# Mixture-of-experts start-up: the first unit's tokens by products with slot marks inside the router

## The reference

```python
def hierarchical_moe(h, w_rg, b_rg, w_re, b_re, w_e_gate, w_e_up, w_e_down):
    """h (T,D) -> (T,D). Top-1 group, then top-2 experts inside the chosen group."""
    p_grp = softmax(h @ w_rg + b_rg); g_sel = argmax(p_grp)
    le = (h @ w_re + b_re).reshape(T, N_GROUPS, E_PER_GROUP)   # 4 groups of 8
    top_p, top_e = top_k(softmax(le[g_sel]), 2)
    w_tok = p_g * top_p / sum(top_p)
    # every expert's tokens are packed into blocks of 128 rows, each block with one expert
    ys = (silu(xb @ w_e_gate[e]) * (xb @ w_e_up[e])) @ w_e_down[e]   # per block
    # out = sum over a token's two picks of weight * ys[row of the pick]
```

## Time and profile before

| what | value |
|---|---|
| three runs | 2894.31, 2905.34, 2900.13 us, median 2900.13 |
| the profiled execution | 2899.79 us, its span 2896.8 us |
| granted TensorE clock over the span | 0.943 |
| TensorE busy | 2591.6 us (89%) |
| VectorE busy | 2064.4 us (71%) |
| ScalarE busy | 926.9 us (32%) |
| GpSimd busy | 406.4 us (14%) |

### The profile page before, as it was taken

The page is one execution under the profiler, slowest core; times in us unless marked ns, Lnnn a source line. Parts: engine busy times, 40 slices in busy tenths (PEclk is TensorE's granted clock), DMA queues, the critical chain, the costliest instruction groups (busy, mean ns, idle before and its releaser), DMA issues. The chain is left out here.

```text
span 2896.8 us, 41643 instructions
## 1 busy us (share of the span) xinstructions
PE 2591.6 (89%) x16631; PEld 1948.6 (67%) x16631; DVE 2064.4 (71%) x2805; ACT 926.9 (32%) x981; POOL 406.4 (14%) x214
## 2 busy tenths in 40 slices
PE   5999888888999989998999997998884999999991
PEld 3444888547888754564788875886573788888870
DVE  6581576688777638536877666985755899999983
ACT  2201111122221013432222103333212777777761
POOL 1000000100000010000000000000001366666642
PEclk8999899899999999999999998999995999999995
DMA  5210222316664271201666323321305899999962
GB/s 190 87 59 18 80 91 76 133 52 189 181 195 132 87 237 65 73 30 58 201 184 183 129 87 108 88 87 44 145 14 221 309 364 367 365 362 356 357 238 104
DMA packets 241821, 459.57 MB, mean 159 GB/s; under 512 B 31398, under 2 KB 193726, under 8 KB 226329
## 3 DMA queue, kind: packets, MB, share of 16 engines
q1 hardware_dynamic: 220344, 432.09, 42.8%
q0 software_dynamic: 14368, 23.79, 2.4%
q10 hardware_dynamic: 6978, 1.80, 0.3%
HBM read 457.50 MB, written 30.56 MB: 168 GB/s over the span
## 5 line engine op out<-in xcount | busy, mean ns | idle before, releaser
L49 PE MATMUL ffn_bank<-ffn_xT_high,ffn_wi_high 128*128 128x512 f32 x704 | 278.4, 395 | 8.9 <-DVE ffn_wi_low L43 5.3
L50 PE MATMUL ffn_bank<-ffn_xT_low,ffn_wi_high 128*128 128x512 f32 x704 | 277.7, 394 | 0.0
L398 DVE SCALAR_TENSOR_TENSOR ffn_nsum<-ffn_nw,ffn_cond,ffn_nsum 128x256 f32<-128x256 f32 x336 | 162.9, 485 | 12.0
L2953 POOL DMA_INDIRECT expert_rows<-exp_ys,exp_to_row x32 | 155.7, 4867 | 45.1 <-issue 44.3
L49 PEld LDWEIGHTS ffn_bank<-ffn_xT_high,ffn_wi_high 128*128 128x128 f32 x704 | 134.0, 190 | 39.2 <-DVE ffn_wi_low L43 6.0
L43 DVE TENSOR_TENSOR moe_g_low<-moe_g,exp_g_high 128x4096 fp32r<-128x4096 f32 x32 | 141.6, 4426 | 25.7 <-ACT exp_g_high L3027 25.7
L50 PEld LDWEIGHTS ffn_bank<-ffn_xT_low,ffn_wi_high 128*128 128x128 f32 x704 | 133.6, 190 | 28.1
L43 DVE TENSOR_TENSOR moe_u_low<-moe_u,exp_u_high 128x4096 fp32r<-128x4096 f32 x32 | 141.6, 4425 | 13.5 <-ACT exp_u_high L3027 13.5
L3027 ACT CAST exp_g_high<-moe_g 128x4096 fp32r<-128x4096 f32 x32 | 116.4, 3636 | 105.1 <-PE exp_p_g L51 79.5
L49 PE MATMUL ffn_bank<-ffn_wo_high,ffn_act_high 128*128 128x512 f32 x352 | 137.8, 392 | 4.8 <-DVE ffn_wo_low L43 4.8
L43 DVE TENSOR_TENSOR moe_d_low<-moe_d,exp_d_high 128x4096 fp32r<-128x4096 f32 x32 | 141.4, 4419 | 0.0
(11 more groups left out here) (646 smaller groups left out, 6217.9 us busy)
## 6 DMA issues: line engine op xcount, KB each, us to landing
moe_g<-in_w_e_gate SPq DMA_DIRECT2D x32, 2048.0 KB, 9.6
moe_u<-in_w_e_up SPq DMA_DIRECT2D x32, 2048.0 KB, 9.9
moe_d<-in_w_e_down SPq DMA_DIRECT2D x32, 2048.0 KB, 9.6
ffn_nw<-in_ada_w SPq DMA_DIRECT2D x24, 1024.0 KB
ffn_nw<-in_w_ada SPq DMA_DIRECT2D x24, 1024.0 KB
stay_z<-in_ffn_w_in SPq DMA_DIRECT2D x44, 512.0 KB, 5.2
ffn_wi<-in_ffn_w_in SPq DMA_DIRECT2D x44, 512.0 KB, 5.3
ffn_wo<-in_ffn_w_out SPq DMA_DIRECT2D x44, 512.0 KB, 3.3
```

Source lines behind the costliest of these rows:

```text
L49: nc.tensor.matmul(out, w[0], x[0], start=start, stop=False, **kw)
L50: nc.tensor.matmul(out, w[0], x[1], start=False, stop=False, **kw)
L398: nc.vector.scalar_tensor_tensor(out=total, in0=nw[:, b, k, :], scalar=cond[:, k:k + 1], in1=total, op0=ALU.mult, op1=ALU.add).then_inc(s[ ...
L2953: nc.gpsimd.indirect_dma_start(ys_dram, bass.IndirectOffsetOnAxis(ap=to_row[h][:, 0, 1:2].bitcast(U32), axis=0), ys[h][:, :], None, bounds ...
```

## The change

The first unit of the expert loop no longer reads the table or gathers its tokens. The router makes them: with `LANES` holding 0 to 127 in each row, VectorE marks in `tokens_of[:, t, s]` whether token p of tile t has slot s, for each pick; TensorE multiplies the modulated tokens (still in SBUF) with the marks, which gives the first 128 slots' tokens already transposed (`bank[6]`, `bank[7]`); ScalarE copies them to `xT`, VectorE makes the halves. The first gate weight's high half is taken by ScalarE behind the router's activations, its low half by VectorE between the second and third logits. The tiles involved now outlive the router: `g_high` shares its address with `xn`, `xT` with `xT_low`. In the expert block the first unit's waits are satisfied by marks (small memsets with an increment) and by one transpose that nobody reads; one row load, one gather, and the first unit's copies and halves are gone.

```diff
-    row = np.concatenate([8 - np.arange(PER_GROUP), 4 - np.arange(GROUPS), np.arange(UNITS)])
+    row = np.concatenate([8 - np.arange(PER_GROUP), 4 - np.arange(GROUPS), np.arange(P)])
...
+        xn, g_high = keep.shared(("xn", [P, NT, D], F32), ("g_high", [P, KD, D_EXP], F32R))
+        xT_high = keep.sb("xT_high", [P, KD, P], F32R)
+        xT, xT_low = keep.shared(("xT", [P, KD, P], F32), ("xT_low", [P, KD, P], F32R))
...
+            pe.wait_ge(s["first_found"], 1)
+            for k in range(KD):
+                for t in range(NT):
+                    last = nc.tensor.matmul(bank[6 + k // 4][:, (k % 4) * P:(k % 4 + 1) * P], h[:, t, k:D:KD], tokens_of[:, t, :],
+                                            start=(t == 0), stop=(t == NT - 1))
+                if k % 4 == 3:
+                    last.then_inc(s["first_psum"], 1)
...
+            act.wait_ge(loaded["g"][0], 16)
+            nc.scalar.copy(first_unit["g_high"][:, :, :], raw["g"][0][:, :, :]).then_inc(s["g_high"], 1)
             act.wait_ge(s["exp_in"], 1)
...
+            for j in range(2):
+                act.wait_ge(s["first_psum"], j + 1)
+                nc.scalar.copy(first_unit["xT"][:, 4 * j:4 * j + 4, :].rearrange("p k n -> p (k n)"), bank[6 + j][:, :]).then_inc(s["first_taken"], 1)
...
             for t in range(NT):
+                if t == 2:
+                    dve.wait_ge(s["g_high"], 1)
+                    low_half(nc.vector, low["g"][0][:, :, :], raw["g"][0][:, :, :], first_unit["g_high"][:, :, :]).then_inc(s["g_split"], 1)
                 dve.wait_ge(s["lg_psum"], t + 1)
...
             nc.vector.tensor_copy(slot[:, :, :], slot_f[:, :, :]).then_inc(s["slots_done"], 1)
+            for t in range(NT):
+                found = ts(tokens_of[:, t, :], LANES, slot_f[:, 0, t:t + 1], None, ALU.is_equal)
+            link(found)
+            for t in range(NT):
+                found = nc.vector.scalar_tensor_tensor(out=tokens_of[:, t, :], in0=LANES, scalar=slot_f[:, 1, t:t + 1], in1=tokens_of[:, t, :],
+                                                       op0=ALU.is_equal, op1=ALU.add)
+            found.then_inc(s["first_found"], 1)
...
+            dve.wait_ge(s["first_taken"], 2)
+            nc.vector.tensor_copy(first_unit["xT_high"][:, :, :], first_unit["xT"][:, :, :]).then_inc(s["first_high"], 1)
+            dve.wait_ge(s["first_high"], 1)
+            low_half(nc.vector, first_unit["xT_low"][:, :, :], first_unit["xT"][:, :, :], first_unit["xT_high"][:, :, :]).then_inc(s["first_split"], 1)
+            dve.wait_ge(s["g_split"], 1)
+            dve.wait_ge(s["first_split"], 1)
...
-            for h in range(2):
-                fetch(0, h)
+            fetch(0, 1)
...
-                pe.wait_ge(gathered[h], i * 16 + 16)
+                pe.wait_ge(gathered[h], i * 16 + 16 * h)
...
-            tokens(0, 0)
+            nc.tensor.transpose(p_x[:, 0, 0:P], ident[:, :], ident[:, :]).then_inc(s["x_psum"], 1)
...
-            for h in range(2):
-                act.dma_start(from_row[h][:, 0, :], table_dram[h * P:(h + 1) * P, :]).then_inc(from_loaded[h], 16)
+            act.dma_start(from_row[1][:, 0, :], table_dram[P:2 * P, :]).then_inc(from_loaded[1], 16)
             act.dma_start(rows[:, :, :], table_dram.rearrange("(u p) c -> p u c", p=P)).then_inc(s["rows_loaded"], 16)
-            take_high("g", 0, 0)
             take_high("u", 0, 0)
-            tokens(0)
...
+            for n, name in enumerate(("xT_done", "x_high", "x_split", "g_high", "g_split")):
+                nc.vector.memset(marks[:, n + 1:n + 2], 0.0).then_inc(s[name], 1)
...
-            weights_low(0, 0, "g")
-            split_tokens(0)
             weights_low(0, 0, "u")
```

More of the change, by code:

```diff
@@ L2621, in moe @@
                    "d": w["w_e_down"].rearrange("e (p k) n -> e p (k n)", k=EF)}
+        xn, g_high = keep.shared(("xn", [P, NT, D], F32), ("g_high", [P, KD, D_EXP], F32R))
+        xT_high = keep.sb("xT_high", [P, KD, P], F32R)
+        xT, xT_low = keep.shared(("xT", [P, KD, P], F32), ("xT_low", [P, KD, P], F32R))
+        first_unit = {"xT": xT, "xT_high": xT_high, "xT_low": xT_low, "g_high": g_high}
         with ExitStack() as inner:
             route(nc, Room(nc, inner, "route"), stay, mod, w, earlier_dram, numbers_dram, empty_dram, desc_dram,
-                  h_dram, table_dram, weight, units, raw, loaded, w_views)
+                  h_dram, table_dram, weight, units, raw, low, loaded, w_views, xn, first_unit)
         with ExitStack() as inner:
-            experts(nc, Room(nc, inner, "exp"), raw, low, loaded, w_views, stay, h_dram, table_dram, ys_dram, units)
+            experts(nc, Room(nc, inner, "exp"), raw, low, first_unit, loaded, w_views, stay, h_dram, table_dram, ys_dram, units)
         with ExitStack() as inner:
@@ L2631, in route @@
 def route(nc, room, stay, mod, w, earlier_dram, numbers_dram, empty_dram, desc_dram, h_dram, table_dram,
-          weight, units, raw, loaded, w_views):
+          weight, units, raw, low, loaded, w_views, xn, first_unit):
     shift, scale = mod[3 * D:4 * D], mod[4 * D:5 * D]
@@ L2635, in route @@
     h = room.sb("h", [P, NT, D])
-    xn = room.sb("xn", [P, NT, D])
+    tokens_of = room.sb("tokens_of", [P, NT, P])
     lanes = room.sb("lanes", [P, 3, KD])
@@ L2648, in route @@
     slot = room.sb("slot", [P, PICKS, NT], I32)
-    desc = room.sb("desc", [P, PER_GROUP + GROUPS + UNITS])
+    desc = room.sb("desc", [P, PER_GROUP + GROUPS + P])
     lg = room.sb("lg", [P, NT, ROUTES])
@@ L2672, in route @@
     bank = [room.ps(f"bank{i}", [P, HALF]) for i in range(8)]
-    names = """c_loaded lanes_loaded lanes_done v_loaded b_loaded r_loaded ssq_done root xn_done h_done h_stored table_empty hT_psum hT_done lg_psum exp_in exp_done
+    names = """c_loaded lanes_loaded lanes_done v_loaded b_loaded r_loaded first_found first_psum first_taken first_high first_split g_high g_split ssq_done root xn_done h_done h_stored table_empty hT_psum hT_done lg_psum exp_in exp_done
                e2_in e2_done picks_done rank_psum slots_done scattered steps ones_done"""
@@ L2677, in route @@
     COUNTING = desc[:, PER_GROUP + GROUPS:PER_GROUP + GROUPS + UNITS]
+    LANES = desc[:, PER_GROUP + GROUPS:PER_GROUP + GROUPS + P]
     def along(v, n):
@@ L2855, in _, with experts @@
             link(nc.vector.tensor_copy(units[:, 1, 0:1], u_exp[:, 1, 0:1]))
-def experts(nc, room, raw, low, loaded, w_views, stay, h_dram, table_dram, ys_dram, units):
-    high = {"g": room.sb("g_high", [P, KD, D_EXP], F32R), "u": room.sb("u_high", [P, KD, D_EXP], F32R), "d": [room.sb(f"d_high{i}", [P, EF, D], F32R) for i in range(2)]}
+            dve.wait_ge(s["first_taken"], 2)
[4 more added lines that the diff above has]
+            dve.wait_ge(s["first_split"], 1)
+def experts(nc, room, raw, low, first_unit, loaded, w_views, stay, h_dram, table_dram, ys_dram, units):
+    high = {"g": first_unit["g_high"], "u": room.sb("u_high", [P, KD, D_EXP], F32R), "d": [room.sb(f"d_high{i}", [P, EF, D], F32R) for i in range(2)]}
     from_row = [room.sb(f"from_row{i}", [P, 1, 2], I32) for i in range(2)]
@@ L2866, in experts @@
     xg = [stay["z"][:, i * D:(i + 1) * D] for i in range(2)]
-    xT_high = room.sb("xT_high", [P, KD, P], F32R)
-    xT, xT_low = room.shared(("xT", [P, KD, P], F32), ("xT_low", [P, KD, P], F32R))
+    xT, xT_high, xT_low = (first_unit[n] for n in ("xT", "xT_high", "xT_low"))
     sil = room.sb("sil", [P, D_EXP])
@@ L2874, in experts @@
     ys = [room.sb(f"ys{i}", [P, D]) for i in range(2)]
-    marks = room.sb("marks", [P, 4])
+    marks = room.sb("marks", [P, 6])
     p_x = room.ps("p_x", [P, 2, HALF])
```

## The result

The changed kernel takes 2882.75 us (median; before 2900.13), ratio 0.9942 with an interval of 0.9925 to 0.9958. Twice more, beside later experiments, it came out at 0.9958 (0.9943 to 0.9973) and 0.9953 (0.9934 to 0.9972). So the gain is 13 to 17 us where 9.3 were forecast, at the very edge of the stated range (its lower end was 2883, and the three medians are 2882.75, 2883.8 and 2882.35). The reasons need to be looked at: the profiled executions differ by 19.8 us of span.

The account below looks back on a forecast made before the run. TensorE, busy 89% of 2896.8 us, bounds the kernel; its unbroken run starts 11.0 us earlier from block start, less 1.7 for the later block: 9.3 saved, 2899.79 to 2890.5 us profiled. Range 2883 to 2899.

Parts of the forecast that it names:

- The expert block: From expert block start to the second unit's first gate product: 19.3 us instead of 30.33, so 11.0 us earlier.
- The router's hidden parts: In the router, gate weight's halves (3.60 and 4.42 us) and marks' delay of unit numbers (4.8 us) hidden under other work.
- The products: Router's 32 plain fp32 products, 64 records: 10.1 us, 25 at 0.216 and 39 at 0.12; block starts 1.7 us later.
- the upper bound of 13.8: Router products with all 64 records at the slow clock, 0.216 us each: 13.8 us.
- The rest of the program: From the second unit on TensorE runs unbroken, save one 6.7 us wait; each microsecond earlier start saves one in total.
- A: Router products at full pace from the first, 7.7 us, hidden; gain 11.0 us, 2888.8; chance 0.15.
- B: Router products slow throughout, 13.8 us; block 5.4 us later, gain 5.6 us, 2894.2; chance 0.22.
- C: Router's table comes later than the tokens, 3 us at most, scatters slowed beside VectorE; gain 8.0, 2891.8; chance 0.10.
- D: Router products serialise through strided weights and one accumulating bank: 24.6 us or more, kernel loses 5.2, 2905; chance 0.05.
- E: In the expert block TensorE stands before the up product, delaying the second unit; gain 7.2 us, 2892.6; chance 0.10.

Follow-up runs that it names:

- x3: The changed kernel with the router products' stationary operand read as 128 neighbouring columns of h, so other tokens for the first unit; 2879.41 us, 0.994.
- x2: The changed kernel with 32 bytes free ahead of xT_high and 32 behind xT_low; 2894.18 us, 0.9991 against the kernel before.
- y1: The changed kernel with every eighth column of h copied by ScalarE to neighbours in hT, read by the router's products; 2875.74 us, 0.9932.

## Why the prediction came out as it did

**The expert block: right.** 11.0 us were forecast from block start to second unit, 10.96 measured. Gate release 8.77 (8.7), up product 8.98 (9.0), second unit 19.37 (19.3). Only the gate product's own start, 1.05 against 0.6, was early on paper; it shows nowhere, as the stretch after it was shorter.

**The router's hidden parts: right.** The gate's halves cost nothing. Cast to first product 2.2 us (2.1 for the marks). The halves of the tokens ended 2.7 us behind the products (2.6) and the barrier took 1.5 (1.67).

**The products: wrong.** "5.4 us hold 25 records at 0.216, and the other 39 at 0.12 take 4.7": the clock rose 4.6 us into these products (5.3 in x3), so that part was nearly right, but the records took 0.24 at either level. 15.5 us lies even above the upper bound of 13.8, because both bounds came from rows whose stationary operand has neighbouring columns; the only strided rows, the transposes, are another kind of instruction. The logits' 0.198 was also misread as a pace at 1.2 GHz: the trace has their first dozen records 0.112 us apart at a granted clock of 1.00 and the rest 0.213 apart at 0.50, so the width of 36 or 128 columns made no difference, and the clock was not "at 0.50 whenever the router's TensorE resumes". The products cost 5.4 us more than forecast and made the block begin 7.0 us late instead of 1.7.

**The rest of the program: "a microsecond by which TensorE's unbroken run begins earlier is a microsecond of the whole time".** Nothing here speaks against it, but I had taken the run itself for unchanged. It was 9.2 us shorter, 7 to 8 of them since the tiles that now outlive the router brought the stationary operands to a multiple of 64 bytes. The forecast had no line for what an allocation moves. Two errors of opposite sign, 5 and 9 us, leave 4 us in the kernel's favour: the stages sum to 13.1 us, and with the scatter of the medians the result stands at the lower end of 2883 to 2899. That it came so near is luck. Of the gain that was reasoned out, 9.3 us, the stages leave 3.9; 7 to 8 of the 13.1 come from a place that nobody chose, and 1.1 from the clock in the last down product.

**The rivals.** A (products hidden) and B (slow clock throughout) are both out: the clock rose as the transposes said. C is in the trace, but small: the second scatter took 2.30 us and the table's last issue came 11.3 us behind the cast, not 10.7, 9.6 us too early to matter. D named the right suspect, strided weights, with the wrong size: 0.24 a record is below the 0.30 at which the sign turns. Without the place (x2) the change is near to nothing. E did not happen: TensorE waited 0.3 us in front of the up product.

## What to carry to other kernels

Where two chains end together in front of an engine, price the removal of each alone as well as of both: here the weight's halves alone were worth 0 in the block, the tokens alone 3.0, both together 11.0. Give a plain fp32 product's stationary operand neighbouring columns, if an engine with time to spare can reorder it; here that was worth 5.5 us from the cast to the block. And when tiles change their room, compare the start addresses of the operands that the busiest loop reads: 32 bytes decided 7 to 8 us, more than the 3.9 of the edit itself.

## What the runs showed of the hardware that was not expected

- With the stationary fp32r operand 32 bytes off a multiple of 64 (206368, 206432, 156768), products of 512 columns took 393 to 396 ns each (medians of the records); at a multiple (206400, 156736) 389. For aT, 216608 gave 396 and 216640 389. Moving tiles of 16 KB lay at multiples of 64 in all of them. Offsets of 16 or 8 bytes were not tried, so "a multiple of 64" is the simplest rule that fits these places, not a proven one. It shows in fp32r products with 512 moving columns only: y1's plain fp32 products of 128 columns read hT at 183456, 32 bytes off, and take 9.93 us like x3's, whose h lies at a multiple (164928).
- 64 plain fp32 records of 128 columns: 15.5 us with a stationary stride of 32 bytes, 9.9 with neighbouring columns, with the granted clock at 0.50 for the first 4.6 and 5.3 us. A record every 0.240 or 0.238 us with the stride (0.50, 1.00), every 0.213 or 0.112 without.
- ScalarE's copy of 128x1024 fp32 with that stride on its input took 1.95 us, against 1.01 for one of the same size from PSUM; no run has the copy from SBUF without the stride.
